# Turning the probabilities one step behind the scores in the first mixer's attention

## What is computed

```python
# neighbourhood_attention: the 256 tokens, for each of 4 rows of 64
s_nb = einsum('bqhd,bwkhd->bhqwk', qr, kb) * scale + bias      # all 256 keys, masked to a window of columns
s_cx = einsum('bqhd,bchd->bhqc', qr, k_ctx) * scale            # 256 context keys, no bias
p = softmax(concatenate([s_nb, s_cx], axis=-1))                # over 512
out = p_nb @ vb + p_cx @ v_ctx
# context_attention: the 256 context tokens on themselves
s = einsum('bqhd,bkhd->bhqk', q, k) * dh ** -0.5
out = softmax(s) @ v
...
y = concatenate([a_out, b_out], axis=-1) @ w_out
```

## Time and profile before

| | us |
|---|---|
| median of 3 runs | 2553.57 (2553.43 to 2554.41) |
| time of the profiled execution | 2553.91 |
| its span | 2552.1 |
| TensorE busy in the span | 2494.1 (98%) |
| VectorE busy | 1990.8 (78%) |
| ScalarE busy | 1175.3 (46%) |
| 16 DMA engines, mean | 236 GB/s |

### The profile page before, as it was taken

One profiled execution on the slowest core, in us unless ns is written; L12 is line 12 of the kernel. 1 busy time (PEld: TensorE's weight loads), 2 busy tenths in 40 slices (PEclk: granted clock), 3 DMA queues, 4 the chain that ended last, 5 costly groups with the idle time before them and its releaser, 6 DMA issues.

```text
span 2552.1 us, 41954 instructions
## 1 busy us (share of the span) xinstructions
PE 2494.1 (98%) x16459; PEld 2142.8 (84%) x16459; DVE 1990.8 (78%) x2455; ACT 1175.3 (46%) x1498; POOL 88.1 (3%) x116
## 2 busy tenths in 40 slices
PE   7999999999999999999999899999999999999998
PEld 5877788888889998889999688888888888888886
DVE  3876877777767886758887747888888888889887
ACT  3436200001421005531014737777777777777776
POOL 0100100000000001000002000000000000000000
PEclk9999999999999999999999999999999999999999
DMA  8843454443335454334545025999899999999996
GB/s 334 320 161 131 165 174 167 165 172 116 116 108 219 181 181 141 108 108 170 184 175 197 18 100 207 373 364 375 334 375 363 361 346 374 366 350 359 363 374 251
DMA packets 91398, 602.75 MB, mean 236 GB/s; under 512 B 9840, under 2 KB 12912, under 8 KB 24688
## 3 DMA queue, kind: packets, MB, share of 16 engines
q1 hardware_dynamic: 76848, 540.05, 56.0%
q0 software_dynamic: 14400, 60.56, 6.7%
HBM read 598.47 MB, written 2.10 MB: 235 GB/s over the span
## 4 chain that ended last, share of the span: by engine, by line
PE 92%; DVE 5%; ACT 2%; SPq 1%; issue 1%; DMA 1%; DVEq 0%; ACTq 0%
PE bank L1195 12%; PE bank L1198 12%; PE bank L1199 12%; PE bank L2546 8%; PE bank L2550 8%; PE bank L2549 8%; PE bank L2577 4%; PE bank L2581 4%; PE bank L2580 4%; PE bank L542 2%; PE bank L1432 1%; PE bank L1453 1%; PE bank L1443 1%; PE bank L2559 1%; PE bank L1244 1%; PE bank L1245 1%
## 5 line engine op out<-in xcount | busy, mean ns | idle before, releaser
L991 DVE TENSOR_TENSOR ring_part<-ring,arena_part 128x2048 fp32r<-128x2048 f32 x481 | 1080.2, 2275 | 33.1 <-ACT arena_part L1010 15.9
L2902 ACT ACTIVATE arena_part<-ring 128x2048 fp32r<-128x2048 f32 x339 | 647.7, 1920 | 191.0 <-DMA ring<-in_stream 190.1
L1195 PE MATMUL bank<-arena_part 128*128 128x256 f32 (+1 forms) x2040 | 650.3, 319 | 8.3 <-DVE ring_part L991 8.3
L1199 PE MATMUL bank<-arena_part,ring_part 128*128 128x256 f32 (+1 forms) x2040 | 646.7, 317 | 0.0
L1198 PE MATMUL bank<-h_part,arena_part 128*128 128x256 f32 (+1 forms) x1496 | 474.2, 317 | 0.0
L1195 PEld LDWEIGHTS bank<-arena_part 128*128 128x128 f32 x2040 | 388.6, 190 | 39.0 <-issue 12.6
L1199 PEld LDWEIGHTS bank<-arena_part,ring_part 128*128 128x128 f32 x2040 | 388.6, 190 | 25.7
L2546 PE MATMUL bank<-arena_part,h_part 128*128 128x512 f32 x896 | 354.1, 395 | 0.0
L2550 PE MATMUL bank<-arena_part,h_part 128*128 128x512 f32 x896 | 349.6, 390 | 0.0
L2549 PE MATMUL bank<-ring_part,h_part 128*128 128x512 f32 x896 | 348.9, 389 | 0.0
L1299 ACT ACTIVATE arena<-bank 128x256 f32<-128x256 f32 (+1 forms) x66 | 30.1, 455 | 636.7 <-PE bank L1199 635.8
(11 more groups left out here) (378 smaller groups left out, 3077.3 us busy)
## 6 DMA issues: line engine op xcount, KB each, us to landing
ring<-in_stream SPq DMA_DIRECT2D x511, 1024.0 KB, 4.9
arena<-in_ada_stream POOLq DMA_DIRECT2D x80, 512.0 KB, 4.6
consts<-in_mem_w POOLq DMA_DIRECT2D x8, 512.0 KB, 4.1
consts<-in_small POOLq DMA_DIRECT2D x1, 2800.0 KB, 11.8
arena<-in_c_rows POOLq DMA_DIRECT2D x2, 1024.0 KB, 8.3
arena<-in_ab_bias POOLq DMA_DIRECT2D x1, 2048.0 KB, 8.6
arena<-in_t_bias POOLq DMA_DIRECT2D x1, 2048.0 KB, 7.9
arena<-in_mem_t SPq DMA_DIRECT2D x1, 1024.0 KB, 5.0
```

The costliest lines, as they stand in the source:

```text
L991: return nc.vector.tensor_tensor(low, value, high.bitcast(F32), ALU.subtract)
L1195: m = nc.tensor.matmul(out_ap, w_high, high, start=start, stop=False)
L1199: return nc.tensor.matmul(out_ap, w_low, high, start=False, stop=stop)
L2902: nc.scalar.activation(high, ring[:, where], ACT.Copy).then_inc(sem("moe_high"), 1)
```

## The change

`order` gets a parameter `behind`: by how many steps T follows S. It was fixed at 2, with V four steps behind S; now V follows by `behind + 2`. The three walks over the first mixer's attention pass `behind=1`, so T follows S by one step and V by three; all other attentions keep 2. The sequence becomes S0, S1, T0, S2, T1, then S(a), V(a-3), T(a-1) for a = 3 to 11, and V9, T11, V10, V11. The instructions themselves, their operands, the buffers and what each of them waits for are the same.

```diff
-        def order(n):
-            for a in range(n + 4):
+        def order(n, behind=2):
+
+            for a in range(n + behind + 2):
                 if a < n:
                     yield "S", a
-                if 0 <= a - 4 < n:
-                    yield "V", a - 4
-                if 0 <= a - 2 < n:
-                    yield "T", a - 2
+                if 0 <= a - behind - 2 < n:
+                    yield "V", a - behind - 2
+                if 0 <= a - behind < n:
+                    yield "T", a - behind
...
-        def attention_pe(book, steps, beside=None):
+        def attention_pe(book, steps, beside=None, behind=2):
             turned, outs = {}, []
-            for what, a in order(len(steps)):
+            for what, a in order(len(steps), behind):
...
-        def attention_act(book, steps, beside=None):
-            for what, a in order(len(steps)):
+        def attention_act(book, steps, beside=None, behind=2):
+            for what, a in order(len(steps), behind):
...
-        def attention_dve(book, steps, beside=None, scale_last="S"):
+        def attention_dve(book, steps, beside=None, scale_last="S", behind=2):
...
-            for what, a in order(len(steps)):
+            for what, a in order(len(steps), behind):
...
-            attention_pe(bk, ab_steps(), values_ready)
+            attention_pe(bk, ab_steps(), values_ready, behind=1)
...
-            attention_act(bk, ab_steps())
+            attention_act(bk, ab_steps(), behind=1)
...
-            attention_dve(bk, ab_steps())
+            attention_dve(bk, ab_steps(), behind=1)
```

## The result

| | us |
|---|---|
| changed kernel, median of 6 runs | 2561.13 (2556.87 to 2566.49) |
| kernel before, median of 6 runs beside it | 2553.9 (2553.36 to 2554.9) |
| ratio | 1.0027, 95% interval 1.0016 to 1.0038 |
| profiled execution of the changed kernel | 2557.4, span 2555.6 |

It is slower by 0.27%, 7.2 us by the medians; the forecast was 2559.2 in a range of 2557.6 to 2562.7, with 0.68 for slower.

What follows compares the result with a forecast made beforehand. TensorE was taken to bound the attention's middle, handovers between engines its two ends. Start +3.67, middle +4.19 and end -2.23 gave +5.63 us; 2553.57 + 5.6 made 2559.2 us, range 2557.6 to 2562.7.

Steps and rivals of the forecast that it cites:

- The loop: First mixer's attention, S4 to S11: S, VectorE's fills, reciprocal, T, next S wait in turn; 27.91 against 23.72 us, +4.19.
- the clean row: TensorE's restart after a wait: T starts 0.22 us after VectorE's reciprocal starts, shown cleanly just once (180.52 to 180.74).
- the bound of 0.27: Upper bound for TensorE's restart behind a reciprocal, from T1 (184.28 to 184.55); in ten places the sum is 6.1 us.
- The misleading row: T1 at 184.55 is shown released by VectorE's reciprocal of step 2; what ended late was ScalarE's copy of T0.
- The start and the end: Attention's two ends: S4 at 189.22 against 185.55, +3.67 us; from S11 to the output product 8.90 against 11.13, -2.23.
- the shorter drain: End of the attention, behind S11: one V and one T fewer stand there, giving back 2.23 us.
- Rival 1: Attention's middle: V(a-3) covers the way to the reciprocal, so every T follows at once; 2553.0 us, chance 0.06.
- Rival 2: At the way into the feed-forward, 250 to 300 us: up to 1.6 us is absorbed; 2557.6 us, chance 0.12.
- Rival 3: In the attention, TensorE's clock falls to 1.2 GHz; ten us of it cost +3.5, 2562.7 us, chance 0.10.
- one row of before: Attention's start, 180 to 184 us: TensorE busy 2.82 of 4 us at clock 1.00, taken to show no fall.
- The number: Whole kernel: 2559.2 us from the sum put on the median of before, 2553.57 + 5.6; mechanism's own range 2558.7 to 2559.7.

Runs made afterwards that it cites:

- The extra instruction: Changed kernel plus one unused 128x256 VectorE reduction ahead of the reciprocal in each of 12 S: 2564.17 us, ratio 1.004; also tried in the order of before.
- the order of before with the longer S: Kernel before the change plus one unused 128x256 VectorE reduction ahead of the reciprocal in each of 12 S: 2556.09 us, ratio 1.0011.
- the reciprocal ahead of the fills: Changed kernel with VectorE making the reciprocal of step a-1 at the head of S(a), not behind its fills: 2553.6 us, ratio 1.0003.
- The four sets of the changed kernel: Changed kernel, first measurement and three repeats without edit: medians 2561.13, 2561.44, 2559.11 and 2560.37 us.
- filler: Changed kernel with unread constant products on TensorE before T0 and T1: 2559.76 us; before every T but T11: 2557.91, again 2558.17 us.
- values three behind: Kernel before the change with V three steps behind S in place of four, T still two behind: 2560.64 us, ratio 1.0025.

## Why the prediction was right, point by point

- *The loop.* As worked out: S4 predicted at 189.22, came at 189.19; S4 to S11 27.91 against 27.87; S11 to the end 8.90 against 8.97 (T11 5.42 behind S11 and not 5.32, since ScalarE's factor ahead of the copy is one of 256 columns here, which takes 0.26 in place of 0.15). With all starts 0.06 later for reasons that lie before the attention, the sum is 5.57 and not 5.63. The restart of TensorE was 0.21 to 0.23 at every T, so the clean row was right and the bound of 0.27 not needed. The extra instruction shows it by its own size: paid before every T up to T10 in one order, at the start alone in the other.
- *The misleading row* of T1: with ScalarE's copy of T0 ahead of the exponentials of S2, T1 now waits for VectorE alone. In the order of before with the longer S, the trace puts the same wait down to ScalarE itself (1.58 us).
- *The start and the end.* +3.6 and -2.2 as worked out. The end isn't a gain in waiting, though I called it what the shorter drain gives back: work moved from behind S11 to ahead of it. In all of TensorE's waits of this attention the whole change is 2.9 (with that before S2) against 8.0 us; the other 0.5 of the 5.6 is counted as busy, as the modelled tail of the last instruction ahead of each wait.
- *Rival 1* (covered): refuted by the 0.28 to 0.71 before each T; it is what the reciprocal ahead of the fills brings about.
- *Rival 2* (given back later): refuted. The shift is the same at the output product and at 1404 us, 5.63 and 5.60, past the 1.6 us of waits that I thought might absorb it.
- *Rival 3* (the clock falls): I gave it 0.10, and it happened in two of four traces, at the start, as its place was foreseen. Its price, +3.5 for 10 us, was measured at +3.60, in part by luck: it counted T and S alone, doubled, and those gave 3.0; the other 0.6 came from V0 at the low clock, less the wait that it covered. What failed is its weight: I set the chance by one row of before, 2.82 busy of 4 us at a clock of 1.00, and took the head after for "much like it", when it has 2.16 busy and a single wait of 1.99. By the traces it should have been near even. The Trainium skill, "TensorE: Matmul & The Clock Gate", part 1, says that idling lowers the clock and activity gives it back; against that rule I had set the row, and two of the four traces agree with the rule.
- *The number.* 2559.2 was made of the loop alone. The four sets of the changed kernel have medians from 2559.11 to 2561.44, so it is low by about 1 (the median of all 28 runs is 2560.1). The falls of the clock in the attention (0, 0, 1.4 and 3.6 us in four traces) have the size that is missing. That they are what is missing is not shown: of the five longest executions, all with a mean clock of 0.989 or 0.990, only one was traced.

What stays open: where the longer executions with filler lose their 4 us, and what brings on the falls, in the attention and in other stages, that come in some executions of a program and not in others.

## What to carry to other kernels

When a group of work is moved closer to the one that feeds it, look on the feeding engine at what stands ahead of the hand-over in its own order: here a reciprocal of 0.16 us stood behind 1.2 us of fills for the next step, and moving it ahead turned +5.6 us into nothing. A pipeline distance that has no wait in it has nothing to give; shortening it moves work from the drain to the start. And a wait of TensorE should be priced with the clock: behind a wait of 2.0 us it fell, and cost 1.4 and 3.6 us more, in two of four traced executions, and a single trace, or the shortest run, won't show it.

## What the runs showed of the hardware

The granted clock fell to 0.50 less than 1 us after a single wait of 1.99 us, ahead of which TensorE had been busy without a gap for over 10 us, and in other executions of the same program with the same wait it didn't. The length of the wait alone doesn't tell: the clock stayed at 1.00 behind waits of 1.84 us (reciprocal first) and 2.26 us (values three behind), and fell at 680 us (extra instruction, order of before) with no wait in the 8 us ahead of it. In the low state T took 1.90 in place of 1.03 us and S 2.01 in place of 1.06, while VectorE's and ScalarE's instructions kept their durations. The falls near 1410 and 1500 us lasted 6.8 to 10.4 us and 0 to 6.8 us in the traces of before and after; between the two traces of before they are worth 2.85 us of the whole time (106.02 against 103.17 us between the same two rows).
